# A bidirectional SSD scan: one decay block a head and chunk, and two wide products across the chunks

## The reference, cut to what matters

```python
def step(state, inp):
    xc, ac, dtc, bc, cc = inp
    cum = jnp.cumsum(ac, axis=1)
    seg = cum[:, :, None] - cum[:, None, :]
    decay = jnp.exp(jnp.where(mask, seg, -jnp.inf))
    scores = jnp.einsum('btgn,bsgn->btsg', cc, bc)
    y_intra = jnp.einsum('btsg,btsgr,bsgr,bsgrp->btgrp', scores, decay, dtc, xc)
    y_state = jnp.einsum('btgn,bgrpn,btgr->btgrp', cc, state, jnp.exp(cum))
    last = cum[:, -1]
    w_end = jnp.exp(last[:, None] - cum) * dtc
    state = state * jnp.exp(last)[..., None, None] + jnp.einsum('bsgn,bsgr,bsgrp->bgrpn', bc, w_end, xc)
    return state, y_intra + y_state
y = y_fwd + y_bwd + d_skip[:, None] * xs
```

## Time and profile before

| | |
|---|---|
| median of 3 runs | 2797.76 us (2797.67 to 2798.13) |
| profiled execution | 2797.92 us, span 2796.2 us |
| mean granted clock of TensorE | 0.982 of full |
| PE busy | 2601.4 us (93%) |
| PE weight loads busy | 2269.0 us (81%) |
| DVE busy | 2140.2 us (77%) |
| ACT busy | 1354.1 us (48%) |
| POOL busy | 781.6 us (28%) |
| the eight scans (first scores to the end of the slabs) | 1293 to 2047 us of the span |
| DMA | 679.62 MB, mean 243 GB/s |

### The profile page before, as it was taken

How to read it: one execution, slowest core, us unless ns; L and a number is a source line. 1 busy time by engine, 2 the same in 40 slices (tenths; PEclk the granted TensorE clock), 3 DMA queues, 4 the chain that set the end, 5 groups by cost and what they waited for, 6 DMA issues and landing times. The chain is left out here.

```text
span 2796.2 us, 45031 instructions
## 1 busy us (share of the span) xinstructions
PE 2601.4 (93%) x14956; PEld 2269.0 (81%) x14956; DVE 2140.2 (77%) x2597; ACT 1354.1 (48%) x2038; POOL 781.6 (28%) x714
## 2 busy tenths in 40 slices
PE   0399999999999999999999899999989999999998
PEld 0288888888888888878888788888878888888887
DVE  6988889886978879986777787778799555555554
ACT  2244444544444444465555544556454444444454
POOL 3522225442434434530111031111345111111123
PEclk9899999999999999999999999999999999999999
DMA  8888889686878879945554485555559555555554
GB/s 331 306 321 318 316 330 363 239 315 229 331 287 314 316 280 324 358 168 196 166 166 166 158 311 207 167 166 165 204 215 338 192 188 188 188 188 188 189 188 142
DMA packets 171670, 679.62 MB, mean 243 GB/s; under 512 B 18672, under 2 KB 35312, under 8 KB 146704
## 3 DMA queue, kind: packets, MB, share of 16 engines
q1 hardware_dynamic: 171488, 677.75, 68.6%
q0 software_dynamic: 48, 0.13, 0.0%
HBM read 675.58 MB, written 2.23 MB: 242 GB/s over the span
## 5 line engine op out<-in xcount | busy, mean ns | idle before, releaser
L1121 DVE TENSOR_TENSOR wl<-raw,wh 128x1024 fp32r<-128x1024 f32 x862 | 1130.0, 1311 | 461.6 <-ACT wh L674 459.7
L918 PE MATMUL psm<-hcat,wh 128*128 128x512 f32 x3984 | 1270.0, 400 | 16.0 <-DVE pad L1279 10.8
L674 ACT ACTIVATE wh<-raw 128x1024 fp32r<-128x1024 f32 x866 | 911.0, 1052 | 215.8 <-PE psm L921 141.4
L921 PEld LDWEIGHTS psm<-hcat,wl 128*128 128x128 f32 x3984 | 755.4, 190 | 179.6
L918 PE MATMUL psm<-hid,wh 128*128 128x512 f32 x2528 | 797.7, 397 | 10.2 <-POOL hid L558 5.7
L921 PE MATMUL psm<-hcat,wl 128*128 128x256 f32 x3984 | 788.7, 280 | 0.0
L918 PEld LDWEIGHTS psm<-hcat,wh 128*128 128x128 f32 x3984 | 613.7, 191 | 19.3 <-issue 13.2
L921 PEld LDWEIGHTS psm<-hid,wl 128*128 128x128 f32 x2528 | 476.4, 188 | 112.5
L921 PE MATMUL psm<-hid,wl 128*128 128x256 f32 x2528 | 497.7, 278 | 0.0
L1134 DVE CUSTOM_DVE_ANT_0 adat<-adat,cond 128x2048 f32<-128x2048 f32 x176 | 427.0, 2426 | 21.1 <-DMA adat<-in_ada 13.8
L918 PEld LDWEIGHTS psm<-hid,wh 128*128 128x128 f32 x2528 | 386.4, 189 | 12.0 <-POOL hid L558 7.0
(11 more groups left out here) (174 smaller groups left out, 1684.7 us busy)
## 6 DMA issues: line engine op xcount, KB each, us to landing
raw<-in_w SPq DMA_DIRECT2D x866, 512.0 KB, 4.2
adat<-in_ada SPq DMA_DIRECT2D x176, 1024.0 KB, 6.4
xs<-in_ada SPq DMA_DIRECT2D x8, 1024.0 KB, 6.7
zs<-in_ada SPq DMA_DIRECT2D x8, 1024.0 KB, 6.2
dec<-running_sums SPq DMA_DIRECT2D x32, 256.0 KB, 5.3
normt<-running_sums SPq DMA_DIRECT2D x16, 256.0 KB, 4.7
adat<-running_sums SPq DMA_DIRECT2D x16, 256.0 KB, 5.3
x<-in_xT SPq DMA_DIRECT2D x1, 2048.0 KB, 17.1
```

Of the source, the lines that this page charges most:

```text
L674: act.activation(wh[:, h % 4, :], raw[:, h % 4, :], ACT.Copy).then_inc(hi_done, 1)
L918: pe.matmul(bank[:, :], wh[:, h % 4, (k + i) * P:(k + i + 1) * P], src[:, kb + i, :], start=(kb + i == 0), stop=(kb + i == KB - 1), skip_g ...
L921: mm = pe.matmul(bank[:, T:2 * T], wl[:, h % 4, (k + i) * P:(k + i + 1) * P], src[:, kb + i, 0:T], start=False, stop=(kb + i == KB - 1), s ...
L1121: dve.tensor_tensor(wl[:, h % 4, :], raw[:, h % 4, :], wh[:, h % 4, :].bitcast(F32), ALU.subtract).then_inc(lo_done, 1)
```

## The change

Each head and chunk keeps one 128x128 decay block. It is the product of the exponential e^-|difference of sums|, which serves both directions within the chunk, and a mask block that holds scores times dt: above the diagonal with dt of one direction, below with the other. ACT makes the exponential and the lower part (four and four instructions of 128x128 a piece), DVE adds the upper part (four scalar_tensor_tensor) and multiplies (two products of 128x256). PE multiplies each head's block once a chunk: four products of 64 columns a piece instead of twelve.

The terms from one chunk to the other are taken for all eight heads at once: x times `far_in` (on POOL, two products of 128x512), two products on PE of 512 columns with the unmasked scores, and the result times `far_out` on DVE in slot 6, which then adds the two parts into `ytok` (ACT's two copies go). `far_in`, `far_out` and the gaps are made once in group 0, on DVE and ACT, before `DT_ALL`; `columns_of` goes. The `em` tiles have 4 x 256 columns and lie elsewhere, so the adaLN tiles are no longer held back (`resume` goes).

```diff
-DT_AV, DT_TOK, DT_CUM, DT_ALL = 11, 13, 14, 15
+DT_AV, DT_TOK, DT_CUM, DT_FAR, DT_ALL = 11, 13, 15, 22, 24
...
-        dec = sb("dec", [P, 2, 4, 3 * P])
+        dec = sb("dec", [P, 3, 4, T])
...
+        upper, lower = (gf[:, 0:P], gf[:, T:3 * P]), (gb[:, T:3 * P], gb[:, P:T])
...
-        em = [None, normt[:, :].rearrange("p (k t) -> p k t", k=4), dec[:, 0], dec[:, 1]]
-        em.append(adat[:, 1, 0:6 * T].rearrange("p (k t) -> p k t", k=4))
+        em = [None, hv, dec[:, 0], dec[:, 1], dec[:, 2]]
+        columns = normt[:, 4 * T:6 * T].rearrange("p (n d h) -> p n d h", n=4, d=2)
+        far_in, far_out, gapS, midS = (columns[:, i] for i in range(4))
...
# POOL, slot 0
-                    for d in (1, 0):
...
-                        src, dst = (xd[:, i, :, :].rearrange("p c (h e) -> p c h e", e=HD) for i in (0, d))
-                        pool.tensor_tensor(dst, src, dgrp[:, :, d, :].unsqueeze(3).to_broadcast([P, 2, HG, HD]),
+                    pool.wait_ge(dt_dve, DT_ALL)
+                    for d in range(2):
+                        src, dst = (xd[:, i, d, :].rearrange("p (h e) -> p h e", e=HD) for i in (0, 1))
+                        pool.tensor_tensor(dst, src, far_in[:, d, heads(g)].unsqueeze(2).to_broadcast([P, HG, HD]),
                                            ALU.mult).then_inc(xd_ready, 1)
...
# ACT, end of group 0, and decays
+            def dt_far():
+                act.wait_ge(dt_dve, DT_FAR)
+                act.activation(far_in, far_in, ACT.Exp).then_inc(dt_act, 1)
+                act.activation(far_out, far_out, ACT.Exp, scale=-1.0).then_inc(dt_act, 1)
...
                 at_least(act, seg_done, g * 4 + piece)
-                for d in range(2):
+                act.wait_ge(dt_dve, DT_ALL)
+                at_least(act, g_ready, g * 4 + 4)
+                for c in range(2):
+                    here = slice(c * P, (c + 1) * P)
                     for i in range(2):
-                        row, h = em[piece][:, 2 * d + i, 0:T], 2 * (piece - 1) + i
-                        ins = act.activation(row, row, ACT.Exp, bias=ngrp[:, d, d, h:h + 1])
+                        own, other = em[piece][:, 2 * c + i, here], em[piece][:, 2 * (1 - c) + i, here]
+                        h = g.c * HG + 2 * (piece - 1) + i
+                        act.activation(own, own, ACT.Exp, bias=ncS[:, c, c, h:h + 1])
+                        ins = act.activation(other, lower[c], ACT.Copy, scale=dtS[:, c, 1, h:h + 1])
...
-                if s == 6:
-                    at_least(act, y_head, g * HG + 2 * HG)
-                    for ch in range(2):
-                        act.activation(ytok[:, ch, :], psy[ch][:, :], ACT.Copy).then_inc(y_tok, 1)
...
# PE, slots 3 to 6
+                    if s == 3:
+                        at_least(pe, g_copied, g * 2 + 2)
+                        at_least(pe, g_ready, g * 4 + 4)
+                        at_least(pe, xd_ready, g * 2 + 2)
+                        pe.matmul(psr[1][:, :], gf[:, P:T], xd[:, 1, 0, :], start=True, stop=True, skip_group_check=True)
+                        pe.matmul(psr[0][:, :], gb[:, 0:P], xd[:, 1, 1, :], start=True, stop=True, skip_group_check=True)
...
-                        for ch, terms in ((0, ((mf, 0, 0, 0), (mb, 2 * P, 1, 0), (mb, 0, 1, 1))),
-                                          (1, ((mf, P, 0, 0), (mf, 2 * P, 0, 1), (mb, P, 1, 1)))):
-                            for i, (m, at, d, sc) in enumerate(terms):
-                                mm = pe.matmul(psy[ch][:, cols], m[:, at:at + P], xd[:, d, sc, cols],
-                                               start=(i == 0), stop=(i == 2), skip_group_check=True)
+                        for ch in range(2):
+                            mm = pe.matmul(psy[ch][:, cols], em[s - 2][:, 2 * ch + h % 2, ch * P:(ch + 1) * P],
+                                           xd[:, 0, ch, cols], start=True, stop=True, skip_group_check=True)
...
# DVE, dt_late at the end of group 0
+                    dve.wait_ge(dt_dve, DT_CUM + 1)
+                    for d in range(2):
+                        own(dve.tensor_tensor(gapS[:, d, :], ncS[:, d, 1 - d, :], ncS[:, d, d, :], ALU.subtract))
+                        own(dve.tensor_tensor(far_in[:, d, :], ncS[:, d, d, :], midS[:, d, :], ALU.add))
+                        own(dve.tensor_tensor(far_out[:, d, :], ncS[:, 1 - d, d, :], midS[:, d, :], ALU.add))
+                    dve.wait_ge(dt_act, 6)
+                    for d in range(2):
+                        own(dve.tensor_tensor(far_in[:, d, :], far_in[:, d, :], dtS[:, d, d, :], ALU.mult))
...
# DVE, masked
-                dve.tensor_tensor(e[:, 0:2, T:3 * P], e[:, 2:4, P:T],
-                                  gf[:, T:3 * P].unsqueeze(1).to_broadcast([P, 2, P]), ALU.mult)
-                dve.tensor_tensor(e[:, 2:4, T:3 * P], e[:, 0:2, 0:P],
-                                  gb[:, T:3 * P].unsqueeze(1).to_broadcast([P, 2, P]), ALU.mult).then_inc(far_done, 1)
...
-                dve.tensor_tensor(e4, e4, gcat[:, :, 0:T].unsqueeze(2).to_broadcast([P, 2, 2, T]), ALU.mult)\
-                    .then_inc(em_ready, 1)
+                for c in range(2):
+                    for i in range(2):
+                        h = g.c * HG + 2 * (piece - 1) + i
+                        other = e[:, 2 * (1 - c) + i, c * P:(c + 1) * P]
+                        ins = dve.scalar_tensor_tensor(out=other, in0=upper[c], scalar=dtS[:, c, 0, h:h + 1], in1=other,
+                                                       op0=ALU.mult, op1=ALU.add)
+                ins.then_inc(sel_done, 1)
+                at_least(dve, sel_done, g * 4 + piece)
+                for c in range(2):
+                    own, other = (e[:, 2 * k:2 * k + 2, c * P:(c + 1) * P] for k in (c, 1 - c))
+                    ins = dve.tensor_tensor(own, own, other, ALU.mult)
+                ins.then_inc(em_ready, 1)
...
# DVE, slot 6
+                if s == 6:
+                    at_least(dve, y_head, g * HG + 2 * HG)
+                    for ch in range(2):
+                        dve.tensor_tensor(ytok[:, ch, :].rearrange("p (h e) -> p h e", e=HD),
+                                          psr[ch][:, :].rearrange("p (h e) -> p h e", e=HD),
+                                          far_out[:, 1 - ch, heads(g)].unsqueeze(2).to_broadcast([P, HG, HD]),
+                                          ALU.mult).then_inc(y_far, 1)
+                    at_least(dve, y_far, g * 2 + 2)
+                    for ch in range(2):
+                        dve.tensor_tensor(ytok[:, ch, :], ytok[:, ch, :], psy[ch][:, :], ALU.add).then_inc(y_tok, 1)
...
-                columns_of(g)
```

More of the change, by code:

```diff
@@ L135, in first_unit, with heads @@
     return g * GU + U_GA
+def heads(g):
+    return slice(g.c * HG, g.c * HG + HG)
 def blocks(g):
@@ L388, in load_half, with load_ada @@
                 sp.dma_start(raw[:, h % 4, :], w[h.v]).then_inc(raw_in[h % 4], 16)
-            def load_ada(a, resumed=False):
-                if not a.terms and (a.c >= ADA or a.c - ADA_OUT0 in (0, 1) and not resumed
-                                    or a.c - ADA_LATE in (0, 1) and not resumed):
+            def load_ada(a):
+                if not a.terms and a.c >= ADA:
                     return
@@ L484, in _ @@
                  lambda: steps(At(U_DT), 1, (), None),
-                 group, late_outs, norm, resume=resume)
+                 group, late_outs, norm)
         @block.gpsimd
@@ L827, in group @@
                         dt_log()
+                    elif s == 9:
+                        dt_far()
             def late_outs(a):
@@ L996, in dt_late @@
                                   start=False, stop=False, skip_group_check=True)
-                        mm = pe.matmul(psr[2][rows, far * P:(far + 1) * P], avS[:, far, rows], up[:, :],
-                                       start=False, stop=True, skip_group_check=True)
+                        pe.matmul(psr[2][rows, far * P:(far + 1) * P], avS[:, far, rows], up[:, :],
+                                  start=False, stop=True, skip_group_check=True)
+                    for near, rows in ((0, f), (1, b)):
+                        mm = pe.matmul(psr[3][:, rows], ones[:, :], avS[:, near, rows], start=True, stop=True,
+                                       skip_group_check=True)
                     mm.then_inc(dt_pe, 1)
@@ L1268, in dt_late @@
                     own(dve.tensor_copy(hv[:, 0, :], psr[2][:, 0:T]))
+                    own(dve.tensor_copy(midS.rearrange("p d h -> p (d h)"), psr[3][:, 0:P]))
                 if s == 9:
@@ L1345, in scan_mid @@
                                                  op0=ALU.mult, op1=ALU.mult).then_inc(gu, 1)
-            def columns_of(g):
-                at_least(dve, dt_dve, DT_ALL)
-                at_least(dve, xd_ready, g * 2)
-                at_least(dve, exp_done, g * 4)
-                for dst, src in ((ngrp, ncS), (dgrp, dtS)):
```

(10 more changed lines are left out.)

30 lines of the change are left out of this document (4 added, 26 removed).

## The result

The changed kernel takes 2846.5 us (median of 4 runs, 2844.1 to 2846.9) beside 2798.0 (2797.7 to 2800.9) for the kernel before: a ratio of 1.0169, 95% interval 1.0152 to 1.0187. That is 48.6 us more, where 9 were forecast and 22 were the top of the range. The sign was right, the size was not. The profiled execution took 2846.9 us, its span is 2845.1.

A forecast was written before the change was run, and what follows sets the result against it. The DVE/ACT chain was taken to bound each group until piece 4, PE after `ytok`; 1.3 + 5.5 + 1.8 - 8.4 + 8.4 = +8.6 us on the profiled 2797.92 gave 2807 us, range 2793 to 2820.

The forecast's parts named there:

- The step that failed: Usual group, slot 5: after splits and taps of 3.86 us and new work of 2.5, `ytok` at 1506.0, transposes 0.25 later.
- POOL's `xd` on the split: Start of a group: shorter `xd` products stretch DVE's segments less, so the first split comes at 1455.4, 3.4 us earlier.
- The clock: After the new 4 us wait before the transposes, slow PE steps cost 1.2 us in seven groups: +8.4; bounds 0 and 1.7.
- The last scan: Inside the output projection PE bounds: it gains 5.4 us and about 3 of a 4.56 us wait, -8.4.
- a ring through DVE and ACT: From a group's start until piece 4, a closed chain through both queues sets the beat: 8.90 us before, 9.56 after.
- Eight ACT instructions: Each piece on ACT: eight 128-column instructions at 0.29 us take 2.35 us, 0.75 more than before.
- The masking: Each piece on DVE: four scalar_tensor_tensor, a hop and two products take 1.84 us, 0.09 less than before.
- the far products: Added on PE in each group: two products of 512 columns, four records taking 1.73 us.
- group 1's chain up to slot 1: Group 1: added small operations, exponentials and products come first, 2 us; slot 1 moves from 1310.53 to 1313.3.
- PE is the bound everywhere: Rival for the whole kernel: all 43 us of removed PE work are gained, 2755 us; chance 5%.
- The ACT instructions are cheap: Rival on ACT: eight instructions take what four took, saving 3 us a group, 21 in seven: 2786 us; chance 8%.
- PE stays at half clock: Rival: six slow steps after the transposes, not three, cost 3.5 us a group, not 1.2: 2823 us; chance 10%.

The follow-up runs named there:

- e1: Changed kernel with the four operations that make `ytok` moved ahead of VectorE's split of slot 6: 2821.2 us.
- e8: Changed kernel with POOL's two products of `xd` with `far_in` made in the first scan only, left out in the other seven: 2833.8 us.
- e7: Changed kernel with 16 unused 128-column matmuls on PE ahead of the slot 7 wait for the sums, in all groups but the last: 2833.2 us.
- e5: Kernel before the change, with each of its four 256-column exponentials of a slot issued as two of 128 columns: 2819.4 us.
- e9: Changed kernel with every head product on PE issued three times, same result: 2848.8 us.
- e13: e11 with every head product on PE issued three times, same result: 2765.0 us.
- e11: e3 with slot 7's transposes between the halves of that unit's weight products, DVE's work on them behind its split, not in the last scan: 2741.3 us.
- e6: Kernel before the change, with its four exponentials of a slot issued ahead of the unit's accumulate and tanh: 2769.1 us.
- e3: Changed kernel with the `ytok` operations ahead of slot 6's split and ACT's decays ahead of accumulate and tanh (slot 0's copies stay behind): 2762.1 us.

## Why the forecast was too low

Between the two traces there are 48.9 us, and they can be placed, with the forecast's own terms beside them (they sum to +8.6, which gives 2806.4 us; 2807 was written):

| stretch | forecast | measured | missed |
|---|---|---|---|
| scores to transposes, groups 1 to 7 | +8.6 | +33.3 | 24.8 |
| transposes to the next scores, the same groups | +8.4 | +16.1 | 7.7 |
| last scan, scores to the next norm sum | -8.4 | -3.0 | 5.4 |
| ahead of the first scores | 0 | +1.5 | 1.5 |
| behind that norm sum | 0 | +0.9 | 0.9 |

**The step that failed** is the one that places `ytok`: "slot 5 at +7.21 = 1499.6; its splits and taps 3.86 and the new 2.5: `ytok` at 1506.0". The four operations were put right behind the taps of slot 5. They are in `scan_mid` of slot 6, and on DVE's queue that is behind the split of slot 6, which in turn waits for ACT's conversion. The work was sized rightly (2.6 us for 2.5), its place in the queue was not, and the wait and the length of the split ahead (2.6 us) stood in no term. In e1's trace the seven transposes come 2.5 to 2.7 us sooner, 18.3 in all, and the last scan is 4.0 shorter. That is 22 of the 40 us missed; the median of e1 says 25.4, and what that holds beyond the 22 is not placed.

**POOL's `xd` on the split.** "I place the first split of the group at 1455.4", 9.0 us after the scores; it starts 9.2 after them (1389.82 from 1380.62). But I priced only the time until POOL was free for the segments and let the split behind them pass at its usual length: 0.85 us more. Slot 1 comes 1.1 us later than forecast. In groups 2, 3, 4, 6 and 7 the transposes miss by 1.1 to 1.3 us more than the placing explains, in group 5 by 0.6, in group 1 by nothing: the 6.5 us left in the first row. The whole of these products costs 12.8 (e8).

**The clock** was priced at 1.2 us in seven groups, 8.4 in all. The stretch behind the transposes is 16.1 longer, 1.4 to 3.0 a group and in five of them outside the bound of 1.7; with fillers six of the seven give back 1.4 to 2.6 us each, 11.8 in all (e7). The kind of cost was right, its size half of what came. The kernel before had a row that spoke for more, and the forecast did not use it: behind the wait of 0.86 us ahead of piece 1 two steps took 1.39 and 1.28 us (from 1472.29).

**The last scan.** "It gains its 5.4, and of the 4.56 us wait about 3". The wait became 2.37, so 2.2 of the 3 came. Of the 5.4 only 0.8 did: PE waits there again, 1.3 us for piece 1 and 2.2 for the sums, which stand behind a split too, and e1 takes 4.0 us out of this scan. The 1.5 us ahead of the first scores lie before anything that the change touches in a scan; over all sixteen traces the first scores start between 1292.2 and 1294.8, in no order of the kernels.

**What held.** The bound was read rightly: a ring through DVE and ACT until piece 4, and not the engine that is 93% busy. Eight ACT instructions take 2.34 us for 2.35 (1395.54 to 1397.88), and e5 gives the term by itself: 2.95 us a group, for 4 times 0.75 = 3.0 by the forecast. The masking (1.85 us for 1.84), the far products (1.73) and group 1's chain up to slot 1 (19.8 us after the scores for 20.2) came as worked out. The rival "PE is the bound everywhere", 2755, is refuted by e9, where 54 us more PE work cost next to nothing. The ranking of engines by occupancy, for PE by its weight loads, that the Trainium skill (Perfetto Trace Analysis, on the most-contended engine) proposes would have misled here, and e13 shows where it holds: once most of the waits are gone. "The ACT instructions are cheap" falls with e5. "PE stays at half clock", six slow steps after the transposes or 3.5 us a group, came about in part: slow were the transposes themselves (1.97 us for 1.09) and one to four steps, 2.3 us a group in the mean. The direction came out right in part by luck: in the sum of +8.6 the last scan's -8.4 and the clock's +8.4 cancel, and neither was right (-3.0 and +16.1).

**What the change is worth.** With the decays ahead in both, e11 against e6: 27.7 us, of the 43 us of PE work that it removes. The waits for pieces, transposes, sums and `pad` come to 26 us in e11 and 12 in e6, which is about what is missing. The two differ in one thing more, since e6 has its transposes where they were; in e6 PE shows no wait at them. Moving them there was not tried.

## What to carry to other kernels

Before pricing an added operation, write down what stands ahead of it in its engine's queue in the place where it is put, and what that waits for; the wait of the neighbour in front is part of its price. If the bound is a closed chain through two in-order queues, first look for work in it that can be issued ahead of the link: that costs no engine any work, and only afterwards is a cut in another engine's work worth its time. To learn whether an engine is the bound in a stage, add work to it there, and look at what the next wait does with it.

## What was not expected

- Tripling PE's head products made a group shorter (71.94 for 72.72 us), since a wait of 3.88 us and the lower clock behind it went away together.
- A wait of 1.4 us in front of the transposes, behind 3.7 us of fillers, was followed by no slow step (eight transposes in 1.09 us); waits of 3.7 us without them were (1.97). Nor is that so every time: in e3 a wait of 3.33 us in group 5 was followed by none (1.09).
- The waits ahead of the pieces alternate, 1.12, 2.84, 1.25 and 2.84 us, though the beat of the pieces is even to 0.03 us. Behind the first wait of 2.84 the unit's matmuls run at the lower clock level for a few steps (1.05 us for two 512-column records at 1413.71, 0.63 otherwise), so PE comes later to the next piece and waits less; behind 1.25 they don't, and the next wait is long again. In e1 a wait of 2.83 was followed by no slow step, so the length of a wait alone does not tell.
